# Latent queries in six full tiles, their rotary rows by DMA, and the row copies of head factors on ScalarE

## The reference

```python
    c_q = rms_norm(q_lat, mla_q_norm)                       # 512 x 256
    q_m = (c_q @ w_q_b).reshape(B, S, MLA_HEADS, MLA_QK_DIM)  # 8 heads of 64 + 32
    q_m = jnp.concatenate([q_m[..., :MLA_NOPE_DIM], apply_rope(q_m[..., MLA_NOPE_DIM:], cos_m, sin_m)], axis=-1)
...
def apply_rope(x, cos, sin):
    half = x.shape[-1] // 2
    x1, x2 = x[..., :half], x[..., half:]
    return jnp.concatenate([x1 * c - x2 * s, x2 * c + x1 * s], axis=-1)
```

## Time and profile before

| | |
|---|---|
| three runs, median (lowest to highest) | 2302.02 us (2300.58 to 2305.23) |
| the profiled execution | 2303.14 us, span 2301.2 us |
| busy share of the span | PE 99%, PEld 71%, DVE 57%, ACT 38%, POOL 9% |
| granted TensorE clock | 0.997 of full speed |
| the chain that ended last | PE 88%, DVE 5%, ACT 3%, DMA 2% |

### The profile page before, as it was taken

How to read it: one execution, slowest core, us unless ns; L and a number is a source line. 1 busy time by engine, 2 the same in 40 slices (tenths; PEclk the granted TensorE clock), 3 DMA queues, 4 the chain that set the end, 5 groups by cost and what they waited for, 6 DMA issues and landing times.

```text
span 2301.2 us, 28354 instructions
## 1 busy us (share of the span) xinstructions
PE 2268.3 (99%) x10904; PEld 1628.7 (71%) x10904; DVE 1322.3 (57%) x2066; ACT 880.2 (38%) x1520; POOL 217.6 (9%) x183
## 2 busy tenths in 40 slices
PE   9999999999999999999999999999999999999998
PEld 7666875444676687544477788888888778888887
DVE  5776644323677664523366757777336665777732
ACT  5575542211457554221143234444223233444422
POOL 0212210000221220100000020000001002000000
PEclk9999999999999999999999999999999999999999
DMA  5301559999430155899953233333333422333331
GB/s 186 96 1 50 212 197 350 409 410 410 158 96 1 47 198 214 340 410 409 410 213 110 74 89 100 95 101 92 101 98 137 113 71 87 108 93 101 101 91 57
DMA packets 112662, 381.63 MB, mean 166 GB/s; under 512 B 16528, under 2 KB 17296, under 8 KB 112272
## 3 DMA queue, kind: packets, MB, share of 16 engines
q1 hardware_dynamic: 108928, 367.05, 45.5%
q0 software_dynamic: 2304, 8.39, 0.9%
q10 hardware_dynamic: 1296, 4.37, 0.5%
HBM read 363.51 MB, written 6.29 MB: 161 GB/s over the span
## 4 chain that ended last, share of the span: by engine, by line
PE 88%; DVE 5%; ACT 3%; DMA 2%; issue 1%; POOL 1%; SPq 0%; POOLq 0%; DVEq 0%; ACTq 0%
PE ps L1405 11%; PE ps L1407 11%; PE ps L1406 11%; PE ps L1726 9%; PE ps L1445 5%; PE ps L1447 5%; PE ps L1446 5%; PE ps L1748 4%; PE ps L1607 3%; PE ps L1466 3%; PE ps L1464 3%; PE ps L1465 3%; PE ps L1557 2%; PE ps L1565 2%; DMA wa<-in_wu 1%; PE ps L1758 1%
## 5 line engine op out<-in xcount | busy, mean ns | idle before, releaser
L2563 DVE TENSOR_TENSOR wlo<-stage,whi 128x1024 fp32r<-128x1024 f32 x260 | 325.9, 1256 | 265.1 <-ACT whi L1871 264.1
L1405 PE MATMUL ps<-hTh,whi 128*128 128x512 f32 x1104 | 434.9, 394 | 0.1
L1407 PE MATMUL ps<-hTh,wlo 128*128 128x512 f32 x1104 | 430.2, 390 | 0.0
L1406 PE MATMUL ps<-hTl,whi 128*128 128x512 f32 x1104 | 430.0, 390 | 0.0
L1871 ACT ACTIVATE whi<-stage 128x1024 fp32r<-128x1024 f32 x260 | 274.1, 1057 | 326.6 <-PE ps L1447 120.7
L1405 PEld LDWEIGHTS ps<-hTh,whi 128*128 128x128 f32 x1104 | 207.3, 188 | 50.6 <-issue 8.2
L1407 PEld LDWEIGHTS ps<-hTh,wlo 128*128 128x128 f32 x1104 | 207.3, 188 | 43.7
L1406 PEld LDWEIGHTS ps<-hTl,whi 128*128 128x128 f32 x1104 | 207.4, 188 | 41.9
L2471 DVE TENSOR_TENSOR ps<-ps,Rs 128x512 f32<-128x512 f32 x124 | 86.0, 698 | 139.6 <-PE ps L1407 125.6
L2474 DVE SCALAR_TENSOR_TENSOR t<-ps,vecs,t 128x511 f32<-128x511 f32 (+1 forms) x176 | 131.1, 745 | 3.7 <-ACT t L1828 0.7
L2471 DVE TENSOR_TENSOR x<-x,ps 128x512 f32<-128x512 f32 x184 | 116.4, 680 | 28.5 <-PE ps L1447 18.0
(11 more groups left out here) (395 smaller groups left out, 4217.1 us busy)
## 6 DMA issues: line engine op xcount, KB each, us to landing
stage<-in_wpk SPq DMA_DIRECT2D x268, 512.0 KB, 3.6
wa<-in_wd SPq DMA_DIRECT2D x56, 512.0 KB, 15.5
wa<-in_wu SPq DMA_DIRECT2D x54, 512.0 KB, 15.3
wa<-in_wg SPq DMA_DIRECT2D x46, 512.0 KB, 15.0
ws<-in_wg SPq DMA_DIRECT2D x26, 512.0 KB, 11.7
ws<-in_wu SPq DMA_DIRECT2D x24, 512.0 KB, 10.4
wr<-in_wg SPq DMA_DIRECT2D x24, 512.0 KB, 15.4
stage<-in_wd SPq DMA_DIRECT2D x22, 512.0 KB, 16.5
```

The source lines that it names most:

```text
L1405: pe.matmul(o, h, ah, start=k == 0, stop=False)
L1406: pe.matmul(o, h, al, start=False, stop=False)
L1407: t = pe.matmul(o, lo, ah, start=False, stop=k == 7)
L2563: ve.tensor_tensor(M.wlo[i % NW][:, :], M.stage[i % NSTAGE][:, :], f(M.whi[i % NW][:, :]), ALU.subtract).then_inc(*S.wlo.mark(("w", i)))
```

## The change

Three things change. First, the six-tile form: the 768 columns of the query weight are regrouped when the chunk is split, the 512 plain ones of all heads first, then the 256 rotary ones (four heads of 32 to a tile). Two tiles (`mqr`) make the rotary rows of heads 0 to 3 and 4 to 7, four (`mq`) the plain rows of two heads each. VectorE multiplies a rotary tile with the cosines (`lc`) and with the sines (`ls`), and SyncE brings each head's 32 rows of both to the query tile: eight DMAs per group (`mqr_out`). The first group's are issued in the list behind tile 0, the second group's in the attention, before unit 2. The sines are loaded in eight pieces of 16 rows at the beginning of each layer's mixer, already swapped, and the key's rotary copy is swapped by two DMAs instead of copied by ScalarE. Second, the ticks stand at tiles 1, 3 and 5 instead of 1, 4 and 7. Third, the row copies of the five head tiles (k, q0 to q3) move from VectorE to ScalarE.

```diff
-        for h in range(8):
+        for t in range(6):
             u = self.take()
-            self.do("mq", l, h, u, i0, i1)
+            self.do("mq" if t > 1 else "mqr", l, t - 2 if t > 1 else t, u, i0, i1)
             self.drop(u)
-            if h in (1, 4, 7):
+            if t == 0:
+                self.do("mqr_out", l, 0)
+            if t in (1, 3, 5):
                 self.tick()
...
+            if n == 2:
+                self.do("mqr_out", l, 1)
...
+    def latq_in(self, t):
+        x = t[:, :].rearrange("p (h c) -> p h c", h=8)
+        return x[:, :, 0:64], x[:, :, 64:96]
...
+        elif name == "rows":
+            l, tile, rb, past = a
+            if tile not in HEADS:
+                continue
+            col, n = COL[tile]
+            q.wait_ge(*S.pool.at("pow", l, tile))
+            if past:
+                q.wait_ge(*S.pe.at("turned", *past))
+            copy(M.tmp[4 + rb][:, :].rearrange("p (a f) -> p a f", a=NT * n),
+                 M.st[:, col:col + NT * n].unsqueeze(2).to_broadcast([128, NT * n, 128 // n]), ("rows", l, tile))
...
+        elif name == "sines":
+            l, = a
+            if l:
+                all_before(q, S, "mixer", l)
+            for g in range(4):
+                for h in range(2):
+                    r = slice(32 * g + 16 * h, 32 * g + 16 * h + 16)
+                    sp.dma_start(M.sin4[r, :], M.dram["rope1"][2][112 - 16 * h:128 - 16 * h, :]).then_inc(
+                        *S.sines.mark(("sines", l)))
...
+        elif name == "mqr_out":
+            l, t = a
+            q.wait_ge(*S.dve.at("mqr", l, t))
+            for g in range(4):
+                r = slice(32 * g, 32 * g + 32)
+                sp.dma_start(M.mq[64:96, 4 * t + g, :], M.lc[t][r, :]).then_inc(*S.mqr[t].mark(("mqr", l)))
+                sp.dma_start(M.mq[96:128, 4 * t + g, :], M.ls[t][r, :]).then_inc(*S.mqr[t].mark(("mqr", l)))
...
         elif name == "mq":
-            l, h, u, i0, i1 = a
-            q.wait_ge(*S.pe.at("mq", l, h))
-            stt(M.mq[64:128, h, :], M.ps[u[0]][64:128, :], 96 ** -0.5, M.mcs[64:128, :], ALU.mult, ALU.mult, ("mq", l, h),
-                ("free",) + u)
+            l, p, u, i0, i1 = a
+            q.wait_ge(*S.pe.at("mq", l, p))
+            ts(M.mq[0:64, 2 * p + 1, :], M.ps[u[0]][64:128, :], 96 ** -0.5, ALU.mult, ("mq", l, p), ("free",) + u)
+        elif name == "mqr":
+            l, t, u, i0, i1 = a
+            q.wait_ge(*S.pe.at("mqr", l, t))
+            q.wait_ge(*S.sines.at("sines", l))
+            stt(M.lc[t][:, :], M.ps[u[0]][:, :], 96 ** -0.5, M.cos4[:, :], ALU.mult, ALU.mult)
+            stt(M.ls[t][:, :], M.ps[u[0]][:, :], 96 ** -0.5, M.sin4[:, :], ALU.mult, ALU.mult, ("mqr", l, t), ("free",) + u)
```

More of the change, by code:

```diff
@@ L1078, in __init__ @@
         self.sing = at("sing", OC + 1408 + 2 * KB, [128, 512])
-        self.mcs = at("mcs", OC + 1408 + 4 * KB, [128, 512])
+        self.cos4 = at("cos4", OC + 1408 + 4 * KB, [128, 512])
+        self.sin4 = A("sin4", 54 * KB, [128, 512])
+        self.lc = [A(f"lc{t}", (68, 56)[t] * KB, [128, 512]) for t in range(2)]
+        self.ls = [A(f"ls{t}", (70, 58)[t] * KB, [128, 512]) for t in range(2)]
         oc = OC + 1408 + 6 * KB
@@ L1488, in pe_program @@
             else:
-                q.wait_ge(*S.dve.at("rows", l, tile))
+                q.wait_ge(*(S.act if tile in HEADS else S.dve).at("rows", l, tile))
                 r = M.tmp[4 + rb] if rb < 2 else M.t2[2]
@@ L1502, in pe_program @@
             t.then_inc(*S.pe.mark(("turn_v", l)))
-        elif name == "mq":
-            l, h, u, i0, i1 = a
+        elif name in ("mq", "mqr"):
+            l, t, u, i0, i1 = a
+            r = slice(128 * t, 128 * t + 128) if name == "mq" else slice(512 + 128 * t, 640 + 128 * t)
             o = claim(u)[:, :]
@@ L1511, in pe_program @@
                 q.wait_ge(*S.dve.at("lo", ("cq", l), k))
-                hh, ll = (w[i % NW][:, h * 128:(h + 1) * 128] for w in (M.whi, M.wlo))
+                hh, ll = (w[i % NW][:, r] for w in (M.whi, M.wlo))
                 pe.matmul(o, hh, ah, start=k == 0, stop=False)
                 pe.matmul(o, hh, al, start=False, stop=False)
-                t = pe.matmul(o, ll, ah, start=False, stop=k == 1)
-            t.then_inc(*S.pe.mark(("mq", l, h), ("w", i0), ("w", i1)))
+                last = pe.matmul(o, ll, ah, start=False, stop=k == 1)
+            last.then_inc(*S.pe.mark((name, l, t), ("w", i0), ("w", i1)))
         elif name == "mk":
@@ L1984, in act_program @@
                     q.wait_ge(*S.mk[m].at("mk", l))
+            elif kind == "mix" and g in (1, 3):
+                q.wait_ge(*S.mqr[g // 2].at("mqr", l))
             copy(PT[g % len(PT)][:, :, qt * 128:(qt + 1) * 128],
@@ L2562, in dve_program @@
                 q.wait_ge(*S.pe.at("e", i // 38 - 1, 177))
+            if i in LATQ:
+                w, x, h = M.latq(M.wlo[i % NW]), M.latq_in(M.stage[i % NSTAGE]), M.latq(M.whi[i % NW])
+                ve.tensor_tensor(w[0], x[0], f(h[0]), ALU.subtract).then_inc(*S.wlo.mark())
+                ve.tensor_tensor(w[1], x[1], f(h[1]), ALU.subtract).then_inc(*S.wlo.mark(("w", i)))
+                continue
             ve.tensor_tensor(M.wlo[i % NW][:, :], M.stage[i % NSTAGE][:, :], f(M.whi[i % NW][:, :]),
@@ L2625, in dve_program @@
             l, tile, rb, past = a
+            if tile in HEADS:
+                continue
             col, n = COL[tile]
@@ L3111, in __init__ @@
         self.mk = [signal(f"key_rope{p}", 16) for p in range(4)]
+        self.mqr = [signal(f"query_rope{t}", 16) for t in range(2)]
+        self.sines, self.kswap = signal("sines_in", 16), signal("key_swap", 16)
         self.dup = [signal(f"key_dup{g}", 16) for g in range(2)]
```

46 lines of the change are left out of this document (30 added, 16 removed).

## The result

The changed kernel took 2308.05 us (median of 20 runs, 2304.84 to 2318.2), the kernel before 2303.46 us (20 runs, 2300.58 to 2307.71): a ratio of 1.0021, 95% interval 1.0014 to 1.0027, so +4.8 us (3.2 to 6.2). The prediction was 2303.7 us, +1.7 on the 2302.02 of the three runs then known. Timed again later, the changed kernel had 2306.31 us (12 runs) against 2304.27: 1.0007, interval 0.9992 to 1.0021, +1.6 us (-1.8 to +4.8). Differences are given by the ratio of the timed runs; the difference of two medians can lie up to 1.5 us from it.

What follows compares the result with a forecast made beforehand. TensorE was 99% busy, with VectorE's in-order queue and the swaps close behind; per layer -2.73 - 1.15 + 3.05 + 0.1 + 1.4 + 0.2 = +0.87 us, +1.7 for both, on 2302.02: 2303.7 us, range 2301 to 2306 (8 in 10: 2299 to 2307.5).

Steps and rivals of the forecast that it cites:

- Two tiles fewer, hole gone: TensorE's latent queries: 12 matmuls less, -2.73 us, and no hole before q3's factors, -1.15 us, per layer.
- Rival B: TensorE gets all it is relieved of, -3.88 us per layer, -7.8 in all: 2294.3 us; chance 0.07.
- The hold-up by SyncE: Eight copies at 0.60 us ahead of the swap of q2 put it at 86.3 instead of 84.84, 1.5 us late.
- rival A: New copies issue in 0.40 us or less, the swap of q2 stays at 84.84: -1.3 us, 2300.7; chance 0.12.
- Rival C: New copies issue at 0.8 us or more on SyncE: +4.9 us in all, 2306.9; chance 0.14.
- VectorE gets the data at 90.1: Swapped halves of q2 reach VectorE at 90.1 instead of 88.65; TensorE stands +3.05 us before the second value tile.
- the forecast's 98.5: First exponential due at 98.5 us in layer 0, against 97.68 in the kernel before.
- 9 matmuls, 2.05 us, and a restart of 0.1: TensorE's work behind its stand at the second value tile, giving scores at 94.6, 0.7 earlier than 95.31.
- stand of 1.4 us before the first transpose: TensorE, done with four score tiles at 98.0, waits until 99.35 to transpose probabilities: +1.4 us per layer.
- The sum: Per layer -2.73 - 1.15 + 3.05 + 0.1 + 1.4 + 0.2 = +0.87 us; both layers +1.7 us.
- The term of 0.2 in the sum: Last term of the per-layer sum, +0.2 us, after the +1.4 us before the first transpose of probabilities.

Runs made afterwards that it cites:

- e6: Kernel before, still eight tiles, with the head factors' row copies on ScalarE and the rotation of q2 behind the last latent-query products: -2.1 us against the kernel before.
- e5: Changed kernel with VectorE's rotation of q2 moved behind the four key copies, SyncE unchanged: -3.7 us against the kernel before.
- e3: Kernel before, still eight tiles, with only the row copies of the five head factors moved from VectorE to ScalarE: -0.9 us against the kernel before.
- e12: e5 with the rotation of q3 also one turn later on VectorE, behind the first maximum: 2296.05 us, -8.1 us against the kernel before.
- e1: Changed kernel with the first group's eight rotary-row copies issued behind the swap of q2 instead of ahead of it: +1.8 us against the kernel before.
- e8: Changed kernel with the first group's eight copies issued from ScalarE's queue instead of SyncE's: -0.7 us against the kernel before.
- e9: Changed kernel again, unedited, timed and profiled: 2306.31 us (12 runs), +1.6 us against the kernel before.
- e11: Changed kernel again, unedited, one profiled run: 2306.76 us.
- e2: Changed kernel with the first value tile's three matmuls computed five times over, twelve matmuls more per layer: +3.9 us against the kernel before.
- e7: Kernel before with nine more matmuls in one projection of layer 0, 2.0 us put in: +2.5 us against the kernel before.
- e4: Changed kernel with the row copies of the head factors back on VectorE, six tiles kept: +3.2 us against the kernel before.

## Why the prediction was wrong

The chain was right; its sum was too small, and the comparison had noise that the range did not hold. Of the 4.4 us between 2303.7 and 2308.05, 1.4 come from the base, 1.2 from the sum, and some 1.7 from neither.

- **Two tiles fewer, hole gone: right.** TensorE had no hole before q3's factors and was ready for the second value tile at 89.24 (89.01 and 0.23; forecast 89.4). That almost none of it reaches the end was right too: 0.1 to 0.3 us per layer for the tiles between e6 and e5, and in e3 0.47 of the 1.15 us of the hole, by way of VectorE's queue. Rival B's -7.8 us needed another order on VectorE; with that order e12 reached -8.1.
- **The hold-up by SyncE: right.** The forecast put the swap of q2 at 86.3, 9.98 us behind the first latent-query matmul; it came at 9.92 to 9.95 in layer 0. The issues lie 0.63 apart, not 0.60, and the first began earlier. Moving them away (e1) or off the queue (e8) takes the stand of layer 0 from 3.3 us to 0.8 and 1.5. So rival A is out. Rival C's 2306.9 is near the result, but its cause did not occur.
- **"VectorE gets the data at 90.1": the step that failed in layer 0.** I carried over 3.81 us from the swap's first issue to VectorE. It took 4.28 to 4.45 in layer 0 of all four profiles of the changed kernel (3.9 in layer 1, behind the same eight copies, so the copies alone do not explain it; the cause stays open). Counted from the first latent-query matmul, the data was due at 13.78 us and came at 14.20 to 14.40 in layer 0. In the first profile SyncE left some 0.4 us between the second and the third of the four issues. In layer 1 three of four profiles had q1's chain 0.4 to 0.6 us later against TensorE, since one issue of q0's swap took 1.07 to 1.19 us; the same four copies in e9 and in the first profile:

```profile
651.98 2.91 SPq L2446 DMA_DIRECT2D sq<-raw  x4
```

```profile
655.01 2.46 SPq L2446 DMA_DIRECT2D sq<-raw  x4
```

  Where neither happened (layer 1 of the first profile) the first exponential came at 22.20, the forecast's 98.5 within 0.02 us, and the stretch grew by 0.84 us (forecast 0.87).
- **"9 matmuls, 2.05 us, and a restart of 0.1": failed, at a small price.** They took 4.0 us in layer 0 of the first profile, 2.3 to 4.0 over the eight stretches. That mattered only where the first maximum then waited for TensorE, some 0.5 us, in three of the eight (the first profile's layer 0, layer 1 of e9 and e11). I first held the clock for the main cause of the long stretch; e2, e9 and e11 refuted it. The forecast's stand of 1.4 us before the first transpose is absent in the first profile, where slow matmuls fill it, and 1.1 us long in layer 0 of e9 and e11.
- **The sum.** The eight stretches average 35.87, +1.46 us per layer for the +0.87 forecast, 2.9 for the kernel instead of 1.7. Of the 0.59 too little, about 0.2 is the clock (three times 0.5 in eight), the rest the late data and the late chain. The term of 0.2 in the sum had no row of its own: it brought TensorE's 0.67 up to the delay of the first exponential, which the trace bears out (that delay plus 13.05 to 13.07 us is the stretch).
- **The comparison.** The base of 2302.02 was the median of three runs; 20 gave 2303.46, which alone is 1.4 us of the miss. The further 1.9 us between the stages' 2.9 and the first timing's 4.8 (the 1.7 above, by ratio) I cannot settle. They go with a lower granted clock: among runs of one of the two kernels 0.001 of clock goes with 1.1 to 1.8 us, so the 0.0015 between the changed kernel's two timings is worth 1.6 to 2.6 us (an estimate from these runs), and its medians lie 1.7 apart. Why the clock was lower the first time is not shown. The profiles do not decide it. Outside the two stages and the last 8 us TensorE was at the lower level for 10 us in the kernel before, for 17, 10, 20 and 10 us in the four profiles of the changed kernel and for 14 us each in e3, e6 and e7. Yet the slow stretch at 616 to 628 is in all four profiles of the changed kernel, in e1, e2, e4, e6 and e8, and not in the kernel before, e3, e7, e5 and e12. A systematic part up to 2 us is not excluded.
- **The range** gave +1.7 about 4 us upward, all for issue costs, none for what a stand of 3 us does or for a base from three runs.

## What to carry to other kernels

An engine that takes its work in order and stands at a transfer delays all that is queued behind it: before taking work off the busiest engine, look what the waiting engine has behind its wait, and put that ahead. Here the change as it stood was a loss, and two rotations moved behind other work turned it into a gain of 8 us on the kernel before, 10 us on the changed one. A time that hangs on one queue's issues should get a margin above the median issue, since one slow issue in the chain cost 0.4 to 0.6 us here. For differences of 0.1%, compare the length of the touched stage across several profiles: it repeated to 0.02 us in the kernel before and e7 (four stretches) and spread over 0.9 us in the changed kernel (eight), where medians of one kernel differed by 1.6 us between timings.

## What the hardware showed unexpectedly

- After stands of 2.97 to 3.48 us TensorE was at the 1.2 GHz level, at once or some matmuls later, in six of eight cases, and like stands of 3.42 and 3.52 us left it at 2.4 GHz. In e4 a stand of 1.88 us had the lower level behind it in layer 1 and not in layer 0. At the lower level matmuls of 512 columns came 0.43 us apart, 0.23 at the upper.
- The clock also fell without a stand: 24 matmuls with one output column each, 2.7 to 3.1 us of unbroken work at 613 to 622 us, had matmuls of 512 columns 0.43 us apart behind them in nine of the fourteen profiles, of six tiles and of eight.
- A copy of 32 rows inside the memory occupies SyncE or ScalarE for 0.59 to 0.61 us in most cases, 0.63 to 0.64 with the gap. Single ones on SyncE took 1.07 to 1.85 us.
